# Last head of an encoder's even layer: four output tiles of head 6 go between and behind the levels of head 7's recurrence

## The chip, the cores and the metric

The kernel runs on one core of a Trainium2 chip. The metric is the device time of one execution in microseconds (us); the number that counts is the median of several runs. The five engines of a core run their own instruction streams and meet only at semaphores: TensorE (PE, with its weight loads shown apart as PEld), VectorE (DVE), ScalarE (ACT), GpSimd (POOL, unused here) and SyncE (SP), which issues the DMA transfers.

## The reference

A sequence of 512 positions with 1024 features passes through one even and one odd layer, in float32:

```python
x = x + even_layer(x); x = x + odd_layer(x); return rmsnorm(x)

def even_layer(x):                       # 8 heads in each of two groups
    proj = rmsnorm(x) @ w_in             # 9 sections of 8 heads x 128 columns
    oa = differential_attention(qa, ka, va) * silu(ga)      # dense, two softmaxes
    ob = hgrn2_bidirectional(qh, ff, fb, ih) * silu(gh)     # gated linear recurrence
    return concatenate([oa, ob]) @ w_out
```

The recurrence decays a state by a gate at every position. Both directions are computed here without a state: decayed query-key products for all pairs of positions, times the values.

## The kernel before

Everything is held transposed: features on the 128 partitions, the 512 positions along the free axis. The residual stream is `xT`, eight tiles of 128x512. Each float32 product that must be exact is made of three fast ones (`split_product`, L74 to L76): both operands are split into a high part (rounded to fp32r) and the rest, and high x high, high x low and low x high are summed in a PSUM bank. ACT makes the high part of each weight (`high`, L569, `high_out`, L575), DVE the low part (`low`, L987, `low_out`, L992).

The even layer runs as an iteration for each head h, 0 to 7, with its order written out by hand on each engine; iteration 0 and iteration 7 (`last`) are written out apart, 1 to 6 are a hardware loop. An iteration does, in PE's order: projections 2 to 6 of head h (`proj`), with the attention scores and the transposes of the softmax mix (`turn_mix` 0 to 3) between them; **the eight output tiles of head h-1** (`out_tiles`: each is y of the recurrence and of the attention times one 128-column slice of w_out, so six matmuls of 512 columns in one PSUM bank, which DVE then adds to `xT`, `add_out`, L863); then head h's recurrence: `diagonal` (L443), the attention's `values` (L415, they need all four `keep_mix` of ACT, L629), `far` (L460), and the seven levels `near_level` 0 to 6 (L468). Each level is a chain through three engines: DVE forms differences of decays (L973 to L976), ACT exponentiates them (`near_decays`, L672), DVE multiplies by the query (`near_scale`, L980), PE makes eight matmuls of 128 columns, and ACT (levels 0 and 1, L682) or DVE (levels 2 to 6, `place_level`, L1003) places the result in `attT`. The banks S[0] and S[1] alternate, so level i also waits until level i-2 is placed. In heads 0 to 6, projections 7 to 10 for the next head stand between the levels. In head 7 there is no next head, and nothing stands there.

After iteration 7 comes head 7's end: `recurrence_values` (L415, attT times the values), its square (ACT L595), the sum over partitions (`sum_squares`, L421), a root (ACT L602, L604), `normalize` (DVE L871), `gate_and_split` (DVE L880, L885, L887, which writes the high and low part of y), head 7's eight output tiles, and with them the squares and their sum for the odd layer's norm (L92 to L106).

In iteration 7 before the change, PE runs turn_mix 3, then output tiles 4 to 7 of head 6, then the diagonal. The tiles use two banks in turn, W (`bank_wide`) and O (`bank_out`); `y`, `o_hi` and `o_lo` are one buffer each, so the split weights of head 7's w_out can't be written until tile 7 of head 6 has read the old ones:

```python
def high_out(h, m):                      # ACT
    act.wait_ge(o_in.sem, o_in.at(h, m + 1))
    if O.full.due(h, 5):
        act.wait_ge(O.full.sem, O.full.at(h, 5))
```

Of the kernel before, what the change touches and what calls it, by code (L numbers as in the profile page):

```python
# [153 lines left out]
def even_layer(nc, w_raw, w_hi, w_lo, wn, rstd, xT, eye, ones, rope, eps, x, w_in, w_out, norm, lam, subln, hgw,  # L154
               rope_d, levels_d, eye_d, w_in_next, norm_next):
    with ExitStack() as ctx:
# [113 lines left out]

        block = ctx.enter_context(nc.Block())
# [85 lines left out]
        def _(pe):  # L357
# [52 lines left out]
            def values(h, use, vals, probsT):  # L410

                if O.free.due(h, use - 1):
                    pe.wait_ge(O.free.sem, O.free.at(h, use - 1))
# [9 lines left out]
            def out_tiles(h, js):  # L423
# [3 lines left out]
                for j in js:  # L427
                    bank, use = (W, j // 2 + 1) if j % 2 == 0 else (O, j // 2 + 2)
                    pe.wait_ge(bank.free.sem, bank.free.at(h, use - 1))
                    for m in range(2):  # L430
                        if m == 1:
                            pe.wait_ge(y_hg.sem, y_hg.at(h, 3))
                        mm = split_product(pe, bank[:], o_hi[:, m, j * P:(j + 1) * P], o_lo[:, m, j * P:(j + 1) * P],
                                           y[:, m, 0], y[:, m, 1], m == 0, m == 1)
# [51 lines left out]
            def iteration(h, first, last):  # L486
# [23 lines left out]
                if not first:  # L510
                    out_tiles(h, range(4, 8))
# [12 lines left out]
                if not last:  # L524
                    proj(h, 8)
                near_level(h, 2)
                near_level(h, 3)
# [16 lines left out]
            sum_squares(HEADS, 0, 1)  # L544
            out_tiles(HEADS, range(8))
# [4 lines left out]
        def _(act):  # L550
# [20 lines left out]
            def high_out(h, m):  # L571
                act.wait_ge(o_in.sem, o_in.at(h, m + 1))
                if O.full.due(h, 5):
                    act.wait_ge(O.full.sem, O.full.at(h, 5))
                act.activation(o_hi[:, m], o_raw[:], ACT.Copy).then_inc(o_high.sem, 1)  # L575
# [14 lines left out]
            def square(h, use, n):  # L590
                act.wait_ge(O.full.sem, O.full.at(h, use))
# [115 lines left out]
            def iteration(h, first, last):  # L707
# [25 lines left out]
                keep_mix(h, 2)  # L733
                silu(h, 6, gate_a)
                act.preload_act_table_set(EXP_LOG)
                keep_mix(h, 3)
# [32 lines left out]
            for j in range(KT):  # L769
                act.wait_ge((W, O)[j % 2].free.sem, (W, O)[j % 2].free.at(HEADS, j // 2 + 1 + j % 2))  # L770
# [5 lines left out]
        def _(dve):  # L776
# [81 lines left out]
            def add_out(h, js):  # L858
                for j in js:
                    bank, use = (W, j // 2 + 1) if j % 2 == 0 else (O, j // 2 + 2)  # L860
                    dve.wait_ge(bank.full.sem, bank.full.at(h, use))
                    dve.wait_ge((W if j % 2 == 0 else O).free.sem, (W if j % 2 == 0 else O).free.at(h, use - 1))
                    dve.tensor_tensor(xT[:, j], xT[:, j], bank[:], ALU.add).then_inc(bank.free.sem, 1)  # L863

            def normalize(h, m):

                use, n, w = (1, 1, w_hg) if m else (6, 2, w_sub)
# [6 lines left out]
            def gate_and_split(h, m):  # L874

                use, gate, count, factor = (1, gate_h, y_hg, 1.0) if m else (6, gate_a, y_da, 1.0 - LAM_INIT)
                dve.wait_ge(O.free.sem, O.free.at(h, use))
# [5 lines left out]
                if O.full.due(h, -1 if m else 5):  # L883
                    dve.wait_ge(O.full.sem, O.full.at(h, -1 if m else 5))
                dve.tensor_copy(y[:, m, 0], yn[:]).then_inc(count.sem, 1)  # L885
# [1264 lines left out]
```

## Time and profile before

| | |
|---|---|
| median of 3 runs | 1221.31 us (1219.17 to 1221.83) |
| the profiled execution | 1219.43 us, its span 1217.5 us |
| busy share of the span | PE 95%, PEld 76%, DVE 78%, ACT 55%, POOL 0% |
| granted TensorE clock, mean | 0.982 of full |
| DMA | 103.07 MB, mean 85 GB/s |
| from turn_mix 3 of head 7 to the start of the odd layer | 687.6 to 743.8 us |

The granted clock is given as a share of full speed: 1.00 is 2.4 GHz, 0.50 is 1.2 GHz. A busy PE is not PE at its peak, because matmuls overlap and their ends are modelled. So the pace of PE is read from the starts of its instructions, not from their durations. Stretches of the timeline are what matters here: it lists the instructions of each engine in order of time, merged where one follows the other without a gap, and behind a row the idle time ahead of it and whose event ended it.

### The profile page before, as it was taken

The numbers are of one execution on the slowest core, as the hardware profiler recorded it, in microseconds if no ns is written. First come the engines' busy times: TensorE is split into PE (matmuls) and PEld (weight loads), VectorE is DVE, ScalarE is ACT, GpSimd is POOL, SyncE is SP. The second block draws the span as 40 slices with busy tenths as digits, with TensorE's granted clock in tenths as the row PEclk, the third lists the DMA queues.
The fourth block names the chain that finished last, engine by engine and source line by source line (L and its number), as shares of the span: only waits on it lengthen the run. The fifth ranks groups of instructions, "written<-read, shape, count | busy, mean of one in ns | idle before, by whom it ended". The sixth has DMA issues, their size and how long they took to land. (4 is left out here: it accounts for less than half of the span.)

```text
span 1217.5 us, 18538 instructions
## 1 busy us (share of the span) xinstructions
PE 1155.3 (95%) x5750; PEld 930.0 (76%) x5750; DVE 953.1 (78%) x1882; ACT 666.4 (55%) x1299; POOL 0.2 (0%) x4
## 2 busy tenths in 40 slices
PE   5989999999999999999999967988999999999996
PEld 3867778778778778787887745877888888888876
DVE  5677779778878878877797777577788788888886
ACT  4355455455554554654555544365666665656663
POOL 0000000000000000000000000000000000000000
PEclk9998999999999999999999988998999999999998
DMA  6522521522423225215215003522432223323111
GB/s 194 142 78 56 130 63 53 138 64 65 129 69 91 86 64 138 65 41 136 69 52 139 18 18 92 121 87 65 120 93 52 86 52 103 89 87 86 52 35 70
DMA packets 131672, 103.07 MB, mean 85 GB/s; under 512 B 5424, under 2 KB 116400, under 8 KB 131632
## 3 DMA queue, kind: packets, MB, share of 16 engines
q1 hardware_dynamic: 131632, 102.54, 30.9%
q8 instruction: 24, 0.39, 0.1%
q14 instruction: 16, 0.13, 0.0%
HBM read 77.36 MB, written 2.10 MB: 65 GB/s over the span
## 5 line engine op out<-in xcount | busy, mean ns | idle before, releaser
L74 PE MATMUL bank_proj<-hH,w_hi 128*128 128x512 f32 x576 | 231.0, 401 | 3.8 <-DVE hL L140 3.8
L76 PE MATMUL bank_proj<-hH,w_lo 128*128 128x512 f32 x576 | 226.2, 393 | 0.0
L75 PE MATMUL bank_proj<-hL,w_hi 128*128 128x512 f32 x576 | 225.6, 392 | 0.0
L74 PEld LDWEIGHTS bank_proj<-hH,w_hi 128*128 128x128 f32 x576 | 109.3, 190 | 26.5 <-issue 5.3
L76 PEld LDWEIGHTS bank_proj<-hH,w_lo 128*128 128x128 f32 x576 | 108.9, 189 | 23.8
L75 PEld LDWEIGHTS bank_proj<-hL,w_hi 128*128 128x128 f32 x576 | 109.3, 190 | 21.6
L74 PE MATMUL bank_odd_proj<-hH,w_hi 128*128 128x512 f32 x288 | 117.2, 407 | 5.1 <-DVE hL L140 4.4
L75 PE MATMUL bank_odd_proj<-hL,w_hi 128*128 128x512 f32 x288 | 113.6, 394 | 0.0
L76 PE MATMUL bank_odd_proj<-hH,w_lo 128*128 128x512 f32 x288 | 113.5, 394 | 0.0
L987 DVE TENSOR_TENSOR w_lo<-w_raw,w_hi 128x1024 fp32r<-128x1024 f32 x73 | 88.8, 1218 | 16.9 <-ACT w_hi L569 16.9
L569 ACT ACTIVATE w_hi<-w_raw 128x1024 fp32r<-128x1024 f32 x75 | 78.9, 1054 | 36.8 <-DMA w_raw<-in_w_in_even 33.1
L1591 ACT ACTIVATE probsT<-bank_odd_turn 128x256 fp32r<-128x256 f32 (+1 forms) x128 | 49.3, 435 | 87.1 <-PE bank_odd_turn L1342 86.9
L1584 ACT ACTIVATE probs<-bank_odd_score,small 128x256 f32<-128x256 f32 (+1 forms) x128 | 66.3, 525 | 53.4 <-DVE small L1809 53.4
L616 ACT ACTIVATE probs<-bank_score,small 128x512 f32<-128x512 f32 x64 | 43.4, 684 | 76.3 <-DVE small L836 76.3
L1816 DVE TENSOR_TENSOR probsT<-bank_odd_turn,probsT 128x256 fp32r<-128x256 f32 (+1 forms) x128 | 56.9, 485 | 26.8 <-ACT probsT L1591 26.0
L74 PEld LDWEIGHTS bank_odd_proj<-hH,w_hi 128*128 128x128 f32 x288 | 55.3, 192 | 16.1 <-DVE hL L140 5.2
L468 PE MATMUL bank_score<-scaled 128*128 128x128 f32 x448 | 60.7, 287 | 4.6 <-DVE scaled L980 2.7
L468 PEld LDWEIGHTS bank_score<-scaled 128*128 128x128 f32 x448 | 58.6, 201 | 8.1 <-DVE scaled L980 3.9
L1327 PE MATMUL bank_odd_score<-ks,qs 128*128 128x256 f32 (+1 forms) x256 | 64.2, 355 | 0.0
L76 PEld LDWEIGHTS bank_odd_proj<-hH,w_lo 128*128 128x128 f32 x288 | 54.6, 190 | 12.3
L75 PEld LDWEIGHTS bank_odd_proj<-hL,w_hi 128*128 128x128 f32 x288 | 55.0, 191 | 9.5
L672 ACT ACTIVATE scaled<-decay 128x1024 f32<-128x1024 f32 x32 | 33.9, 1059 | 47.2 <-PE bank_score L468 45.5
(316 smaller groups left out, 2445.4 us busy)
## 6 DMA issues: line engine op xcount, KB each, us to landing
w_raw<-in_w_in_even SPq DMA_DIRECT2D x72, 512.0 KB, 4.7
w_raw<-in_w_in_odd SPq DMA_DIRECT2D x36, 512.0 KB, 4.9
qs<-parts SPq DMA_DIRECT2D x96, 128.0 KB, 2.3
ks<-parts SPq DMA_DIRECT2D x40, 256.0 KB, 4.3
o_raw<-in_w_out_even SPq DMA_DIRECT2D x16, 512.0 KB, 4.8
o_raw<-in_w_out_odd SPq DMA_DIRECT2D x14, 512.0 KB, 6.7
out<-w_raw SPq DMA_DIRECT2D x8, 256.0 KB, 2.1
mixT<-in_x SPq DMA_DIRECT2D x2, 512.0 KB, 5.5
```

Source lines behind the costliest of these rows:

```text
L74: pe.matmul(out, hi, moving_hi, start=start, stop=False)
L75: pe.matmul(out, hi, moving_lo, start=False, stop=False)
L76: return pe.matmul(out, lo, moving_hi, start=False, stop=stop)
L468: mm = pe.matmul(S[i % 2][:, c * P:(c + 1) * P], scaled[:, i % 2, 0, c * P:(c + 1) * P], scaled[:, i % 2, 1, c * P:(c + 1) * P], start=Tru ...
L569: act.activation(w_hi[s][:], w_raw[s][:], ACT.Copy).then_inc(w_high.sem, 1)
L616: act.activation(probs[:, c], S[c][:], ACT.Exp, bias=neg_max[:, i:i + 1], scale=SCALE, accum_out=row_sum[:, i:i + 1]).then_inc(S[c].free.s ...
L672: act.activation(scaled[:, i % 2], buf(i)[:, :, :], ACT.Exp).then_inc(near_exp.sem, 1)
L987: dve.tensor_tensor(w_lo[s][:], w_raw[s][:], w_hi[s][:].bitcast(F32), ALU.subtract).then_inc(w_low.sem, 1)
L1327: mm = pe.matmul(at, query, keys, start=part == 0, stop=False)
L1584: act.activation(probs[:, t % 2, a, 0:n * P], S[a][:, 0:n * P], ACT.Exp, bias=neg_max[:, i:i + 1], scale=SCALE, accum_out=row_sum[:, i:i + ...
L1591: act.activation(probsT[:, 0, 0:n, a], chunked(T[a][:, 0:n * P]), ACT.Copy).then_inc(probs_high[a].sem, 1)
L1816: dve.tensor_tensor(probsT[:, 1, 0:n, a], chunked(T[a][:, 0:n * P]), probsT[:, 0, 0:n, a].bitcast(F32), ALU.subtract).then_inc(T[a].free.s ...
```

## The change

On PE, in iteration 7, head 6's output tiles 4 to 7 no longer stand ahead of the diagonal. Tile 4 comes between levels 1 and 2, tile 5 between levels 2 and 3, and tiles 6 and 7 behind `sum_squares` of head 7's end. DVE adds tiles 4 and 5 to `xT` between placing levels 3 and 4, and tiles 6 and 7 behind head 7's last `gate_and_split`. Banks: tile 5 goes to PB[1], tile 7 to PB[2], 4 and 6 to W; head 7's own even tiles go to O and its odd ones to W. Since head 6's operands are read longer, head 7 gets other homes: its split w_out goes to the memory of `ks`, `qs` and `parts`, the attention half of its y to `hH[:, 0:2]`; the recurrence half of y stays in `y[:, 1]`, and its writing waits for tile 7 (PB[2].full). ACT's `high_out` waits for the last scores (S[1].full) where it waited for tile 7. In iteration 7 ACT also runs `keep_mix(3)` ahead of `silu` of the attention's gate and of the change of activation tables behind it. SP's queue and the DMAs are as they were.

```diff
@@ -268,6 +268,25 @@
         def buf(i):
             return decay if i % 2 == 0 else soft
 
+        def final(h, first=HEADS - 1):
+            return isinstance(h, int) and h >= first
+
+        def o_use(h, n):
+
+            return n - 2 if final(h, HEADS) or final(h) and n > 3 else n
+
+        def out_bank(h, j):
+
+            if final(h, HEADS):
+                return (O, o_use(h, j // 2 + 2)) if j % 2 == 0 else (W, j // 2 + 1)
+            if final(h) and j >= 4:
+                return {4: (W, 3), 5: (PB[1], 3), 6: (W, 4), 7: (PB[2], 3)}[j]
+            return (W, j // 2 + 1) if j % 2 == 0 else (O, j // 2 + 2)
+
+        last_hi = ks[:, :, :, :].rearrange("p c i t -> p (c i t)").rearrange("p (m d) -> p m d", m=2)
+        last_lo = [tile[:, :, :].rearrange("p i t -> p (i t)") for tile in (qs, parts)]
+        last_y = hH[:, 0:2]
+
         block = ctx.enter_context(nc.Block())
 
 
@@ -409,6 +428,7 @@
 
             def values(h, use, vals, probsT):
 
+                use = o_use(h, use)
                 if O.free.due(h, use - 1):
                     pe.wait_ge(O.free.sem, O.free.at(h, use - 1))
                 for c in range(NC):
@@ -425,13 +445,16 @@
                 pe.wait_ge(y_da.sem, y_da.at(h, 0))
                 pe.wait_ge(o_low.sem, o_low.at(h, 0))
                 for j in js:
-                    bank, use = (W, j // 2 + 1) if j % 2 == 0 else (O, j // 2 + 2)
-                    pe.wait_ge(bank.free.sem, bank.free.at(h, use - 1))
+                    bank, use = out_bank(h, j)
+                    pe.wait_ge(bank.free.sem, bank.free.at(HEADS - 1 if bank in PB else h, use - 1))
+                    cols = slice(j * P, (j + 1) * P)
                     for m in range(2):
                         if m == 1:
                             pe.wait_ge(y_hg.sem, y_hg.at(h, 3))
-                        mm = split_product(pe, bank[:], o_hi[:, m, j * P:(j + 1) * P], o_lo[:, m, j * P:(j + 1) * P],
-                                           y[:, m, 0], y[:, m, 1], m == 0, m == 1)
+                        hi, lo = (last_hi[:, m], last_lo[m]) if final(h, HEADS) else (o_hi[:, m], o_lo[:, m])
+                        part = last_y if final(h, HEADS) and m == 0 else y[:, m]
+                        mm = split_product(pe, bank[:], hi[:, cols], lo[:, cols], part[:, 0], part[:, 1],
+                                           m == 0, m == 1)
                     mm.then_inc(bank.full.sem, 1)
 
             def diagonal(h):
@@ -507,7 +530,7 @@
                 turn_mix(h, 2)
                 proj(h, 6)
                 turn_mix(h, 3)
-                if not first:
+                if not first and not last:
                     out_tiles(h, range(4, 8))
 
                 diagonal(h)
@@ -523,7 +546,11 @@
                 near_level(h, 1)
                 if not last:
                     proj(h, 8)
+                else:
+                    out_tiles(h, [4])
                 near_level(h, 2)
+                if last:
+                    out_tiles(h, [5])
                 near_level(h, 3)
                 if not last:
                     proj(h, 9)
@@ -542,6 +569,7 @@
             iteration(HEADS - 1, False, True)
             recurrence_values(HEADS)
             sum_squares(HEADS, 0, 1)
+            out_tiles(HEADS - 1, [6, 7])
             out_tiles(HEADS, range(8))
             rms_next.sum(pe)
 
@@ -570,9 +598,11 @@
 
             def high_out(h, m):
                 act.wait_ge(o_in.sem, o_in.at(h, m + 1))
-                if O.full.due(h, 5):
+                if final(h):
+                    act.wait_ge(S[1].full.sem, S[1].full.at(h, 4))
+                elif O.full.due(h, 5):
                     act.wait_ge(O.full.sem, O.full.at(h, 5))
-                act.activation(o_hi[:, m], o_raw[:], ACT.Copy).then_inc(o_high.sem, 1)
+                act.activation((last_hi if final(h) else o_hi)[:, m], o_raw[:], ACT.Copy).then_inc(o_high.sem, 1)
 
             def soften(h, d):
 
@@ -588,7 +618,7 @@
                 act.activation(at, at, ACT.Ln, bias=1.0).then_inc(softplus.sem, 1)
 
             def square(h, use, n):
-                act.wait_ge(O.full.sem, O.full.at(h, use))
+                act.wait_ge(O.full.sem, O.full.at(h, o_use(h, use)))
                 act.wait_ge(T.full.sem, T.full.at(h, 7 - 8 if n == 1 else 1))
                 if squared.due(h, n - 1):
                     act.wait_ge(squared.sem, squared.at(h, n - 1))
@@ -731,9 +761,12 @@
                 silu(h, 4, query)
                 silu(h, 5, gate_h)
                 keep_mix(h, 2)
+                if last:
+                    keep_mix(h, 3)
                 silu(h, 6, gate_a)
                 act.preload_act_table_set(EXP_LOG)
-                keep_mix(h, 3)
+                if not last:
+                    keep_mix(h, 3)
                 high_out(h, 0)
                 high(h, 9)
                 square(h, 6, 2)
@@ -767,7 +800,8 @@
             square(HEADS, 1, 1)
             root(HEADS, 0, 1)
             for j in range(KT):
-                act.wait_ge((W, O)[j % 2].free.sem, (W, O)[j % 2].free.at(HEADS, j // 2 + 1 + j % 2))
+                bank, use = out_bank(HEADS, j)
+                act.wait_ge(bank.free.sem, bank.free.at(HEADS, use))
                 rms_next.square(act, j)
             rms_next.root(act)
 
@@ -857,14 +891,15 @@
 
             def add_out(h, js):
                 for j in js:
-                    bank, use = (W, j // 2 + 1) if j % 2 == 0 else (O, j // 2 + 2)
-                    dve.wait_ge(bank.full.sem, bank.full.at(h, use))
-                    dve.wait_ge((W if j % 2 == 0 else O).free.sem, (W if j % 2 == 0 else O).free.at(h, use - 1))
+                    bank, use = out_bank(h, j)
+                    at = HEADS - 1 if bank in PB else h
+                    dve.wait_ge(bank.full.sem, bank.full.at(at, use))
+                    dve.wait_ge(bank.free.sem, bank.free.at(at, use - 1))
                     dve.tensor_tensor(xT[:, j], xT[:, j], bank[:], ALU.add).then_inc(bank.free.sem, 1)
 
             def normalize(h, m):
 
-                use, n, w = (1, 1, w_hg) if m else (6, 2, w_sub)
+                n, w = (1, w_hg) if m else (2, w_sub)
                 dve.wait_ge(rooted.sem, rooted.at(h, n))
                 if (y_da if m else y_hg).due(h, 0 if m else 3):
                     dve.wait_ge((y_da if m else y_hg).sem, (y_da if m else y_hg).at(h, 0 if m else 3))
@@ -874,17 +909,22 @@
             def gate_and_split(h, m):
 
                 use, gate, count, factor = (1, gate_h, y_hg, 1.0) if m else (6, gate_a, y_da, 1.0 - LAM_INIT)
-                dve.wait_ge(O.free.sem, O.free.at(h, use))
+                to = last_y if final(h) and m == 0 else y[:, m]
+                dve.wait_ge(O.free.sem, O.free.at(h, o_use(h, use)))
                 bank, gate_use = bank_of(5 if m else 6)
                 dve.wait_ge(bank.free.sem, bank.free.at(h, gate_use - (3 if m else 0)))
                 dve.scalar_tensor_tensor(out=yn[:], in0=yn[:], scalar=factor, in1=gate[:], op0=ALU.mult,
                                          op1=ALU.mult).then_inc(count.sem, 1)
                 dve.wait_ge(count.sem, count.at(h, 1))
-                if O.full.due(h, -1 if m else 5):
+                if final(h, HEADS):
+                    dve.wait_ge(PB[2].full.sem, PB[2].full.at(HEADS - 1, 3))
+                elif final(h) and m == 0:
+                    dve.wait_ge(PB[2].full.sem, PB[2].full.at(h, 2))
+                elif O.full.due(h, -1 if m else 5):
                     dve.wait_ge(O.full.sem, O.full.at(h, -1 if m else 5))
-                dve.tensor_copy(y[:, m, 0], yn[:]).then_inc(count.sem, 1)
+                dve.tensor_copy(to[:, 0], yn[:]).then_inc(count.sem, 1)
                 dve.wait_ge(count.sem, count.at(h, 2))
-                dve.tensor_tensor(y[:, m, 1], yn[:], y[:, m, 0].bitcast(F32), ALU.subtract).then_inc(count.sem, 1)
+                dve.tensor_tensor(to[:, 1], yn[:], to[:, 0].bitcast(F32), ALU.subtract).then_inc(count.sem, 1)
 
             def rotate(h, n):
 
@@ -989,8 +1029,8 @@
 
             def low_out(h, m):
                 dve.wait_ge(o_high.sem, o_high.at(h, m + 1))
-                dve.tensor_tensor(o_lo[:, m], o_raw[:], o_hi[:, m].bitcast(F32),
-                                  ALU.subtract).then_inc(o_low.sem, 1)
+                hi, lo = (last_hi[:, m], last_lo[m]) if final(h) else (o_hi[:, m], o_lo[:, m])
+                dve.tensor_tensor(lo, o_raw[:], hi.bitcast(F32), ALU.subtract).then_inc(o_low.sem, 1)
 
             def place_level(h, i):
 
@@ -1037,7 +1077,7 @@
                 mixes(h, 3)
                 low(h, 8)
                 far_scale(h)
-                if not first:
+                if not first and not last:
                     add_out(h, range(4, 8))
                 place_diagonal(h)
                 near_differences(h, 0)
@@ -1066,6 +1106,8 @@
                 if not last:
                     low(h, 11)
                     rotate(h, 8)
+                else:
+                    add_out(h, [4, 5])
                 place_level(h, 4)
                 near_scale(h, 6)
                 place_level(h, 5)
@@ -1080,6 +1122,7 @@
             iteration(HEADS - 1, False, True)
             normalize(HEADS, 1)
             gate_and_split(HEADS, 1)
+            add_out(HEADS - 1, [6, 7])
             for j in range(KT):
                 add_out(HEADS, [j])
                 if j >= 2:
```

## Rows read from the trace of the kernel before

**Rows 1.** Windows: length, busy PE, PEld, DVE, ACT, POOL; granted clock; DMA share

```profile
700.00:743.80 43.80, 30.17 (x124) 21.91 (x122) 30.73 (x57) 20.55 (x34) 0.00 (x0) 0.88 0.04 12
...
706.00:708.00 2.00, 1.55 (x7) 1.56 (x8) 2.00 (x6) 1.93 (x5) 0.00 (x0) 0.54 0.00 0
...
716.00:718.00 2.00, 1.43 (x10) 0.97 (x8) 1.35 (x3) 0.67 (x1) 0.00 (x0) 0.90 0.00 0
...
726.00:728.00 2.00, 0.00 (x0) 0.00 (x0) 1.90 (x4) 0.00 (x0) 0.00 (x0) 1.00 0.00 0
```

**Rows 2.** Timeline, PE: turn_mix 3, first matmul of tile 4, diagonal, values

```profile
687.60 0.60 PE L392 MATMUL bank_turn<-eye,mix 128*128 128x128 f32 x4
687.95 0.48 PE L74 MATMUL bank_wide<-y,o_hi 128*128 128x512 f32 x1
...
693.52 1.05 PE L443 MATMUL bank_score<-query,attT 128*128 128x128 f32 x8
...
694.55 3.67 PE L415 MATMUL bank_out<-mixT,v 128*128 128x512 f32 x8
```

**Rows 3.** Timeline, ACT, over the same stretch

```profile
687.79 0.60 ACT L634 ACTIVATE gate_a<-bank_proj 128x512 f32<-128x512 f32 x1 [2.48 <-PE bank_proj L76]
688.41 1.28 ACT L735 ACT_TABLE_LOAD   x1
689.70 0.60 ACT L629 ACTIVATE mixT<-bank_turn 128x512 f32<-128x512 f32 x1
693.77 1.06 ACT L575 ACTIVATE o_hi<-o_raw 128x1024 fp32r<-128x1024 f32 x1 [3.47 <-PE bank_out L76]
...
694.74 1.04 ACT L569 ACTIVATE w_hi<-w_raw 128x1024 fp32r<-128x1024 f32 x1
...
698.26 0.60 ACT L595 ACTIVATE sq<-bank_out 128x512 f32<-128x512 f32 x1 [2.48 <-PE bank_out L415]
```

**Rows 4.** Timeline, DVE: last part of far_scale, placing the diagonal

```profile
686.26 0.87 DVE L950 TENSOR_SCALAR scaled<-scaled,small 128x128 f32<-128x128 f32 x4
...
694.61 0.69 DVE L941 TENSOR_TENSOR attT<-bank_score,eye 128x512 f32<-128x512 f32 x1 [0.20 <-PE bank_score L443]
```

**Rows 5.** Timeline, PE: level 1; levels 2 and 3; levels 4 and 5

```profile
703.84 1.16 PE L468 MATMUL bank_score<-scaled 128*128 128x128 f32 x8 [0.79 <-DVE scaled L980]
...
706.45 4.20 PE L468 MATMUL bank_score<-scaled 128*128 128x128 f32 x16 [1.44 <-DVE scaled L980]
...
712.52 3.76 PE L468 MATMUL bank_score<-scaled 128*128 128x128 f32 x16 [1.88 <-DVE attT L1003]
```

**Rows 6.** Timeline, ACT and DVE between the levels

```profile
705.71 0.68 DVE L980 TENSOR_TENSOR scaled<-query,scaled 128x512 f32<-128x512 f32 x1
...
707.35 1.11 ACT L682 ACTIVATE attT<-bank_score 32x128 f32<-32x128 f32 x4
...
710.74 1.06 ACT L672 ACTIVATE scaled<-soft 128x1024 f32<-128x1024 f32 x1 [1.06 <-DVE decay L973]
...
712.27 0.68 DVE L980 TENSOR_TENSOR scaled<-query,scaled 128x512 f32<-128x512 f32 x1
...
714.67 1.06 ACT L672 ACTIVATE scaled<-decay 128x1024 f32<-128x1024 f32 x1 [2.87 <-PE bank_score L468]
714.75 0.73 DVE L1003 COPY_PREDICATED attT<-level_mask,bank_score 128x512 f32<-128x512 uint8 x1 [1.17 <-PE bank_score L468]
```

**Rows 7.** Timeline: head 7's values, sum of squares, split of y, first adds

```profile
718.62 3.70 PE L415 MATMUL bank_out<-attT,vh 128*128 128x512 f32 x8 [0.96 <-DVE attT L1003]
...
723.10 1.10 PE L421 MATMUL bank_turn<-sq,ones 128*128 128x512 f32 x2 [0.78 <-ACT sq L595]
...
727.13 0.43 DVE L885 CAST y<-yn 128x512 fp32r<-128x512 f32 x1
...
729.34 0.69 DVE L863 TENSOR_TENSOR xT<-xT,bank_wide 128x512 f32<-128x512 f32 x1 [1.05 <-PE bank_wide L76]
...
730.71 0.69 DVE L863 TENSOR_TENSOR xT<-xT,bank_out 128x512 f32<-128x512 f32 x1 [0.69 <-PE bank_out L76]
```

## The prediction

> **What bounds the kernel now.** I looked at the page first: PE is busy 95% of the span, so most of it is a queue of matmuls in which reordering gains nothing. The slices show one hole before the odd layer, and the windows give it an edge: from 700.0 to 743.8 us PE is busy 30.17 of 43.80 us, and DVE and ACT aren't full either [rows 1]. So there the time is set by a chain through the engines, and 13.6 us of PE are free. Just ahead of the hole, PE is full. The timeline of that stretch shows what it is full of: turn_mix 3 from 687.60, head 6's tiles 4 to 7 from 687.95, and only at 693.52 the diagonal with which head 7's recurrence begins on PE [rows 2]. DVE has had its scaled operands ready since 686.26 + 0.87 = 687.13 and waits for the diagonal, which it places at 694.61 [rows 4]. ACT waits 3.47 us for tile 7 [rows 3]. The chain of this stretch is therefore: four tiles on PE, diagonal, values, square, far products, seven levels, head 7's values, square, sum, root, y, eight tiles, norm. Whatever can leave the front of it and fit into its holes is gained whole.
>
> **The front: tiles 4 to 7 leave.** They are 24 matmuls, and their price is the distance of the starts: 693.52 − 687.95 = 5.57 us, 0.232 each, 1.39 a tile [rows 2]. The diagonal moves to 687.95. What could be late there instead:
>
> - DVE has nothing pending after 687.13, so placing the diagonal moves from 694.61 to 689.04 [rows 4]. The adds of tiles 4 to 7 are gone from there too.
> - PE's `values` moves from 694.55 to 688.98 [rows 2] and needs `keep_mix(3)`. In the old ACT order it would wait: the silu, the table change, and then the copy, which ends at 689.70 + 0.60 = 690.30 [rows 3], 1.3 us late. In the new order the copy comes first. The transposes end at 687.60 + 0.60 = 688.20 [rows 2], so it runs from about 688.24 to 688.84: 0.1 us ahead of need.
> - Behind it ACT runs the silu (0.60), the table change (1.28), the split of head 7's w_out (its successor starts 694.74 − 693.77 = 0.97 later) and the split of a weight of the odd layer (1.04), and then the square, which PE's values now want at 698.26 − 5.57 = 692.69 [rows 3]. From 688.73 that is: silu to 689.35, change to 690.63, split to 691.61, split to 692.65. It just fits, with nothing to spare: 0 us, and each 0.1 us more in this row of five is 0.1 us on the path.
>
> ACT's old wait for tile 7 is replaced by one for the last scores, long past; the homes in `ks`, `qs`, `parts` and `hH` are free then, since head 7 has no next head to rotate and its last projection is done before turn_mix 3. No instruction is added for them. SP issues what it did, with head 7's second w_out load 5.6 us sooner on idle DMAs. The front gives −5.57 us.
>
> **The activation tables, weighed.** The row shows a table change of 1.28 us with the next ACT instruction 0.01 us behind it (688.41 + 1.28 = 689.69, then 689.70) and none but the usual gap ahead of it [rows 3]. The Trainium skill, "ScalarE: Activation LUTs", section "What ACT_TABLE_LOAD costs", gives about 1283 ns for the load and a drain of about 1380 ns beside it, some 2.66 us for each switch. The load agrees with the trace, the drain does not appear in it. By the page the ACT row above would be 1.38 us longer and the gain only about 4.2 us; by the row it costs nothing more.
>
> **Tile 4, between levels 1 and 2.** Level 1's eight matmuls start at 703.84 and PE then sits idle 1.44 us until level 2 at 706.45, which waits for DVE's multiply (705.71 + 0.68 = 706.39) [rows 5, 6]. I put these in the old times, all of which move by −5.57. PE can issue the tile at about 703.84 + 1.0 = 704.84 and is through with its issue at 706.23: inside the hole, 0 us.
>
> **Tile 5, between levels 2 and 3.** Level 3 waits for ACT to place level 1 (707.35 + 1.11 = 708.46) [rows 6]. At full clock level 2 is issued by 707.45 and the tile by 708.84, so level 3 is 0.3 us late. Who waits for it: ACT's exponentials of level 5, at 710.74 [rows 6]. Their reader on DVE comes at 712.27 whatever they do, because DVE's differences and a placement stand ahead of it, and they last 1.06: ready at 711.80, 0.47 us of cover. So 0 us. In the old trace levels 2 and 3 took 4.20 us for 16 matmuls at a clock of 0.54 to 0.50 in place of some 2.2 [rows 1, 5]; see the rivals.
>
> **Adds of tiles 4 and 5** are two DVE instructions of 0.69 [rows 7], some 1.3 us issued back to back, ahead of placing level 4. DVE is idle 1.17 us there before [rows 6]; so that placement is 0.1 us late. The next in line, level 6's multiply, waits for ACT's exponentials until 714.67 + 1.06 = 715.73, and the placement ends before it: 0 us.
>
> **Tiles 6 and 7, behind the sum of squares.** Sum_squares ends on PE at 723.10 + 1.10 = 724.20 with its issue done a little sooner [rows 7]. Twelve matmuls at 0.232 take 2.8 us: the last ends at about 727.0. DVE writes the high part of y at 727.13 [rows 7], and it now waits for tile 7: 0.1 us of cover. PE then makes the attention half of head 7's tile 0 (three matmuls, 0.7 us, on bank O, which the normalize has left before the multiply that ends ahead of 727.13) by 727.7, before y is complete at 729.34 − 1.05 = 728.29. Two more adds of 0.69 on DVE start at 728.29, and the first add of head 7's tiles comes at about 729.5 in place of 729.34. The next has 0.69 us of idle time ahead of it [rows 7], which takes this in: 0 to 0.2 us, I take 0.1. Bank W is freed for tile 1 by 728.29 + 0.69 = 728.98, and PE wants it behind the second half of tile 0, at 728.3 + 0.7 = 729.0: just in time.
>
> **Sum.** −5.57 + 0 + 0 + 0 + 0.1 = −5.5 us (rounded) on the profiled execution: 1219.43 − 5.5 = 1213.9. That execution was 1.9 us below the median of the runs, which I take as chance; against the median, **1221.31 − 5.5 = 1215.8 us**.
>
> **Unknowns and their bounds.** What the trace of before doesn't show is how these tiles go with the clock. Before, the clock fell to half in 706 to 708, after PE's thin stretch, and rose in 716 to 718; through 726 to 728, with PE wholly idle, it stayed at 1.00 [rows 1]. With tiles 4 and 5 PE is nearly unbroken from 703.8 to 710, and the first fall should be gone; between level 3's end and level 4's start at 712.52 is a hole of about 2.5 us that stays [rows 5]. The lower bound of cost is full clock throughout: levels 4 and 5 then take 2.3 us (twice 1.16) in place of 3.76 [rows 5]. Level 4 ends 0.7 earlier, but DVE is now the limit, since the adds come first, from 714.75 − 1.17 = 713.58 to about 714.8 [rows 6], and the placement ends at 715.4, 0.35 us ahead of where the multiply began before: about −0.4 us. The upper bound is half clock from level 2 on: level 2 in 1.9, tile 5 in 2.8, level 3 in 1.9, so level 3 ends at 713.0 in place of 710.65, the exponentials of level 5 end 2.3 us late where 0.47 was covered, and what follows catches up in part with DVE's idle 1.17: +1.1 us. Both ends are kept; I take 0, by the row nearest: levels 4 and 5 as slow as before, 2 and 3 faster.
>
> **Rivals.**
>
> 1. *As summed*, −5.0 to −6.1 us, about 1215.8: 0.62.
> 2. *Full clock to the end*: −5.5 − 0.4 and a little from a luckier clock elsewhere, −6.3, 1215.0. For it: no fall in 726 to 728 without any matmul. Against: the fall near 706 with PE still over half busy. 0.12.
> 3. *Half clock in levels 2 to 5 or late into level 6*: −5.5 + 1.1 to + 2.5, so −3 to −4.4, 1217.6. For it: rows 5. 0.13.
> 4. *ACT becomes the front's bound*: the row of five has no slack; if the change of tables costs a drain in its new place, +1.3, so −4.2, 1217.1. Against: the row shows none. 0.05.
> 5. *The tiles don't fit, and the change gives back what it takes*: if PE can't issue tiles 6 and 7 before `normalize` or the sum's bank, they stand on the path with 2.8 us, and tile 5 with 1.4: −1.3, 1220.0, no difference that can be told. Against: the holes were read at 1.44 and, with rows 7, nearly 3 us. 0.05.
> 6. *Slower*: the clock falls in the hole before level 4 and isn't given back until after tiles 6 and 7. Level 6 costs +0.7, the values' 3.70 us double, +3.7, sum_squares +0.9, and the two tiles 5.6 us in place of 2.8, which pushes the high part of y by 2.6: +7.9, so +2.4, and head 7's first tiles more: 1224. It decides from a cost of 5.5, that is from a half clock that lasts until tile 7. Against: the rise at 716 to 718 before the values [rows 1]. 0.03.
>
> **How the numbers follow.** 1215.8 is case 1. Runs of this kernel lie 1.4 us either side of their middle, so 0.2% (2.4 us) is about what can be told from no change. The range runs from full clock with a good draw, 1213.4, to case 3's dear end, 1218.5, and leaves out cases 5 and 6 and a tail at both sides, in all under 0.2. Faster by over 0.2%: cases 1 to 4 whole, 0.92; the same: case 5, 0.05; slower: case 6, 0.03.
>
> **What would show it.** In the changed profile: the diagonal right behind turn_mix 3, and values 1.0 us behind it with no wait for ACT; the square of the attention right at the end of values; level 2 still released by DVE, not by tile 4; DVE's idle time before level 4's placement gone; the high part of y released by ACT's root, not by tile 7; the start of the odd layer near 738.3 in place of 743.8. From turn_mix 3 to there the distance shrinks by 5.5 us and nothing else moves. Wrong it would be by a wait on ACT's copy or square, by level 3 behind tile 5 at half clock, or by the high part of y waiting for PE.

## The result, and the profile after

The changed kernel takes 1212.64 us at the median of six runs (1211.01 to 1215.56), the kernel before 1219.49 us (1219.11 to 1221.83): 6.9 us less, ratio 0.994 with a 95% interval of 0.9925 to 0.9956, so 5.4 to 9.2 us. The forecast was faster, which held, at 1215.8 us with a range from 1213.4, which did not: the measured time lies 0.8 us below its low end. The profiled execution took 1211.01 us with a span of 1209.1, and 8.4 us of span is more than the medians differ by. So the first question to the profile is where the 8.4 us lie. The timeline of PE after, in the rows that answer to [rows 2], [rows 5] and [rows 7]:

```profile
682.83 0.60 PE L411 MATMUL bank_turn<-eye,mix 128*128 128x128 f32 x4
683.26 1.06 PE L466 MATMUL bank_score<-query,attT 128*128 128x128 f32 x8
684.15 3.66 PE L435 MATMUL bank_out<-mixT,v 128*128 128x512 f32 x8
...
696.04 1.16 PE L491 MATMUL bank_score<-scaled 128*128 128x128 f32 x8
...
698.42 1.05 PE L491 MATMUL bank_score<-scaled 128*128 128x128 f32 x8
...
702.00 2.34 PE L491 MATMUL bank_score<-scaled 128*128 128x128 f32 x16 [2.52 <-DVE attT L1043]
...
707.62 5.40 PE L435 MATMUL bank_out<-attT,vh 128*128 128x512 f32 x8 [0.96 <-DVE attT L1043]
713.79 1.10 PE L441 MATMUL bank_turn<-sq,ones 128*128 128x512 f32 x2 [0.78 <-ACT sq L625]
```

The sum of the next norm on PE, and the odd layer's first multiply on DVE, which is the start of the odd layer in the prediction; first the kernel before, then after:

```profile
741.01 1.12 PE L106 MATMUL bank_turn<-rstd,ones 128*128 128x512 f32 x2 [2.18 <-DVE rstd L101]
743.84 1.42 DVE L136 SCALAR_TENSOR_TENSOR soft<-xT,wn,rstd 128x512 f32<-128x512 f32 x2 [2.88 <-PEq L156]
```

```profile
731.72 1.97 PE L106 MATMUL bank_turn<-rstd,ones 128*128 128x512 f32 x2 [2.18 <-DVE rstd L101]
735.40 1.41 DVE L136 SCALAR_TENSOR_TENSOR soft<-xT,wn,rstd 128x512 f32<-128x512 f32 x2 [3.74 <-PEq L156]
```

Read as distances from turn_mix 3 of head 7 (687.60 before, 682.83 after):

| from turn_mix 3 to | before | after |
|---|---|---|
| diagonal | 5.92 | 0.43 |
| attention's values | 6.95 | 1.32 |
| head 7's values | 31.02 | 24.79 |
| its sum of squares | 35.50 | 30.96 |
| the sum of the next norm | 53.41 | 48.89 |
| the odd layer's first multiply (DVE) | 56.24 | 52.57 |

Turn_mix 3 itself comes 4.77 us earlier, in code that the change doesn't touch. From there to the odd layer the stretch is 3.67 us shorter, where the forecast wanted 5.5, and the two make up the 8.4. The front gives 5.63 us by the values, where 5.57 were forecast. By head 7's values it is 6.23 us. Behind them 1.7 is lost again, because those eight matmuls take 5.40 us in place of 3.70, and another 0.85 at the norm's sum, which takes 1.97 us in place of 1.12. The windows say why. From 60 to 105 us (head 0), from turn_mix 3 to head 7's values, and from there to the next norm's sum, first the kernel before, then after; the number ahead of the two of the DMA is the granted clock:

```profile
60.00:105.00 45.00, 39.23 (x159) 28.77 (x158) 31.64 (x69) 26.04 (x51) 0.00 (x0) 0.89 0.28 84
687.60:718.62 31.02, 25.45 (x120) 20.15 (x118) 23.73 (x49) 17.99 (x28) 0.00 (x0) 0.83 0.05 17
718.62:741.01 22.39, 15.99 (x59) 10.67 (x59) 15.14 (x23) 6.97 (x11) 0.00 (x0) 1.00 0.00 1
```

```profile
60.00:105.00 45.00, 38.75 (x184) 29.91 (x183) 34.77 (x75) 27.14 (x52) 0.00 (x0) 1.00 0.28 82
682.83:707.62 24.79, 19.02 (x108) 14.47 (x106) 21.76 (x47) 17.87 (x28) 0.00 (x0) 1.00 0.06 21
707.62:731.72 24.10, 20.45 (x71) 13.51 (x71) 16.23 (x25) 6.98 (x11) 0.00 (x0) 0.93 0.00 1
```

At 0.83 of full over 31.02 us, the clock before was at its lower level, 1.2 GHz, for about 10 us; after, it isn't at all in the levels, and it is for some 3.4 us in head 7's values. Ahead of that fall PE was busy 3.42 us of the 7.5 from 700.0 to 707.5, all at full clock. Some of the rows at half a us, with the fall and the rise, after:

```profile
707.00:707.50 0.50, 0.00 (x0) 0.00 (x0) 0.50 (x2) 0.00 (x0) 0.00 (x0) 1.00 0.00 0
707.50:708.00 0.50, 0.39 (x1) 0.30 (x2) 0.50 (x2) 0.00 (x0) 0.00 (x0) 0.97 0.00 0
708.00:708.50 0.50, 0.50 (x2) 0.18 (x1) 0.50 (x1) 0.00 (x0) 0.00 (x0) 0.50 0.00 0
...
711.00:711.50 0.50, 0.50 (x2) 0.21 (x1) 0.00 (x0) 0.00 (x0) 0.00 (x0) 0.61 0.00 0
```

Head 0, which both kernels run alike, had in 60 to 105 us about 10 us of the lower clock before and none after. Its turn_mix 3, the attention's values and the far products, first before, then after:

```profile
90.57 0.63 PE L392 MATMUL bank_turn<-eye,mix 128*128 128x128 f32 x4 [2.49 <-ACT mixT L629]
...
92.88 6.51 PE L415 MATMUL bank_out<-mixT,v 128*128 128x512 f32 x8 [0.58 <-ACT mixT L629]
99.23 1.91 PE L460 MATMUL bank_score<-scaled 128*128 128x128 f32 x10
```

```profile
88.59 0.63 PE L411 MATMUL bank_turn<-eye,mix 128*128 128x128 f32 x4 [2.54 <-ACT mixT L659]
...
90.90 3.70 PE L435 MATMUL bank_out<-mixT,v 128*128 128x512 f32 x8 [0.79 <-ACT mixT L659]
94.43 1.91 PE L483 MATMUL bank_score<-scaled 128*128 128x128 f32 x10
```

After is 1.98 us ahead at this turn_mix 3 and 4.80 us ahead behind the values. That is a draw, since other runs of the same code show either value (6.50 us in "two between", 3.70 in "homes only"), and it is the whole of the early 4.77 us. The two front steps that had no slack went as forecast; the rows of ACT that answer to [rows 3]:

```profile
683.46 0.60 ACT L659 ACTIVATE mixT<-bank_turn 128x512 f32<-128x512 f32 x1 [2.89 <-PE bank_turn L411]
683.96 0.59 ACT L664 ACTIVATE gate_a<-bank_proj 128x512 f32<-128x512 f32 x1
684.57 1.28 ACT L767 ACT_TABLE_LOAD   x1
685.86 1.06 ACT L605 ACTIVATE ks<-o_raw 128x1024 fp32r<-128x1024 f32 x1
686.82 1.04 ACT L597 ACTIVATE w_hi<-w_raw 128x1024 fp32r<-128x1024 f32 x1
...
687.85 0.60 ACT L625 ACTIVATE sq<-bank_out 128x512 f32<-128x512 f32 x1
```

The copy comes first, the table change is 1.28 us with no drain behind it, and the square starts without a wait. By the Trainium skill's "ScalarE: Activation LUTs", section "What ACT_TABLE_LOAD costs", a drain of about 1.38 us would have delayed it; again no row shows one.

### The profile page after: what moved, and what is told of

Same layout as the page of the kernel before. It is cut to its first block and busy times, and to the rows that moved or that the text cites. A ratio compares the mean times of both kernels' runs of the same rounds, so it can differ in the third digit from the quotient of the medians.

```text
span 1209.1 us, 18540 instructions
## 1 busy us (share of the span) xinstructions
PE 1148.0 (95%) x5750; PEld 923.7 (76%) x5750; DVE 952.1 (79%) x1882; ACT 666.5 (55%) x1299; POOL 0.2 (0%) x4
## 5 line engine op out<-in xcount | busy, mean ns | idle before, releaser
L491 PE MATMUL bank_score<-scaled 128*128 128x128 f32 x448 | 57.3, 276 | 4.8 <-DVE attT L1043 2.5
L491 PEld LDWEIGHTS bank_score<-scaled 128*128 128x128 f32 x448 | 55.5, 191 | 8.3 <-DVE scaled L1020 3.2
```

Of the source, the lines that this page charges most:

```text
L491: mm = pe.matmul(S[i % 2][:, c * P:(c + 1) * P], scaled[:, i % 2, 0, c * P:(c + 1) * P], scaled[:, i % 2, 1, c * P:(c + 1) * P], start=Tru ...
```

## The experiments

The question: is the gain beyond 5.5 us structure that the sum missed, clock, or a draw? One run of "6, 7 behind" took 4030 us, with no known cause; it is in no median and no ratio here. Medians, all against the kernel before on the same chip. Distances are from turn_mix 3 of head 7 in each profile, and each row of the table has one profile.

| kernel | median us (runs) | before us | ratio, 95% interval |
|---|---|---|---|
| homes only | 1217.89 (12) | 1218.14 | 0.9997, 0.9978 to 1.0016 |
| 6, 7 behind | 1213.78 (11) | 1218.14 | 0.9960, 0.9941 to 0.9980 |
| two between | 1215.38 (12) | 1218.14 | 0.9978, 0.9959 to 0.9997 |
| old copy order | 1212.71 (12) | 1218.14 | 0.9951, 0.9931 to 0.9971 |
| before, filled | 1215.54 (11) | 1219.73 | 0.9962, 0.9951 to 0.9973 |
| after, filled | 1209.21 (6) | 1219.73 | 0.9913, 0.9896 to 0.9930 |
| after, filled in head 7 | 1210.29 (6) | 1219.73 | 0.9934, 0.9909 to 0.9958 |
| after, head 0's copies | 1209.38 (6) | 1219.73 | 0.9912, 0.9894 to 0.9929 |
| after again | 1210.01 (6) | 1218.48 | 0.9938, 0.9917 to 0.9959 |
| before, short fillers | 1212.57 (8) | 1218.48 | 0.9953, 0.9937 to 0.9970 |
| after, short fillers | 1207.09 (5) | 1218.48 | 0.9907, 0.9888 to 0.9927 |
| combined | 1205.43 (5) | 1218.48 | 0.9892, 0.9871 to 0.9912 |
| after, short, adds later | 1207.20 (4) | 1218.36 | 0.9910, 0.9883 to 0.9936 |
| combined, adds later | 1206.47 (4) | 1218.36 | 0.9905, 0.9880 to 0.9929 |

**Homes only.** PE and DVE order as before, all else as changed; one of several places:

```diff
-                if not first and not last:
+                if not first:
                     out_tiles(h, range(4, 8))
```

> The changed kernel with tiles 4 to 7 of head 6 back ahead of the diagonal (adds too); new homes, banks, waits and the earlier keep_mix(3) stay. Theory (the gain is the four tiles leaving the front, 5.57 us, plus clock): the same as before, within 0.5 us, apart from the draw of the clock. Rival (the homes themselves or the earlier wait of ACT give a part of the 6.9 us): 1 to 1.4 us faster than before.

No difference in the time that can be told: the interval runs from 2.7 us faster to 1.9 slower, so it does not by itself exclude the rival's 1 to 1.4 us. The profile speaks against the rival: head 7's values are 0.22 us earlier than before (30.80 and 31.02), the next norm's sum 0.61 later (54.02 and 53.41). It shows a price that I had not seen: head 7's tile 0 is on bank O now and waits for the normalize, which leaves PE idle, and here the clock was at its lower level behind that hole (0.53 in 721 to 723 us):

```profile
720.00 0.75 DVE L901 SCALAR_TENSOR_TENSOR yn<-bank_out,w_hg,rstd 128x512 f32<-128x512 f32 x1 [4.15 <-ACT rstd L629]
...
720.90 0.56 PE L74 MATMUL bank_out<-hH,ks 128*128 128x512 f32 x1 [2.32 <-DVE yn L901]
721.26 0.63 PE L75 MATMUL bank_out<-hH,ks 128*128 128x512 f32 x1
```

In the full change tiles 6 and 7 stand there, and 0.69 us of the hole is left.

**Only tiles 6 and 7 behind; only two tiles between.** Tiles 4 and 5 stay ahead of the diagonal; the other two go behind the sum of squares, or between the levels:

```diff
-                if not first and not last:
-                    out_tiles(h, range(4, 8))
+                if not first:
+                    out_tiles(h, range(4, 6) if last else range(4, 8))
```

> Tiles 6 and 7 behind the sum of squares as in the change, tiles 4 and 5 back ahead of the diagonal. Theory: half of 5.57, so 2.8 us faster than before, with levels 2 to 5 at half clock as before. Rival (filling the levels is worth more than the tiles' own time, by the clock): this one gains less than half of what the whole change gains, about 2.5 us.

> Tiles 6 and 7 between the levels, where the change has 4 and 5; tiles 4 and 5 ahead of the diagonal; nothing behind the sum of squares. Theory by issue time alone: 2.8 us faster than before. Rival (clock): 2.8 plus 0.6 to 1 us, since levels 2 to 5 run at full clock; the profile then shows the clock at 1.00 from level 2 to level 3.

The profiles give 2.86 us each at the attention's values (4.09 in place of 6.95), half the front. The times give 4.4 and 2.8 by the medians, 4.9 and 2.7 by the ratios, and add up to the whole. Neither rival is told apart by them; the intervals are 2 us wide each way. The profiles do say something of the second. With two tiles between, levels 2 and 3 ran at full clock (1.16 and 1.05 us), levels 4 and 5 did not (3.46 us for 16 matmuls), and head 7's values are 3.34 us earlier than before, 0.5 more than the half front. By the next norm's sum it is 2.48, since tile 0 waits there as in "homes only"; with 6 and 7 behind it is 3.01. The two add up to 5.49 us.

**The old copy order.**

```diff
-                if last:
-                    keep_mix(h, 3)
                 silu(h, 6, gate_a)
                 act.preload_act_table_set(EXP_LOG)
-                if not last:
-                    keep_mix(h, 3)
+                keep_mix(h, 3)
```

> The changed kernel with keep_mix(3) behind the silu and the table change again. Theory: values wait for the copy, 1.3 to 1.4 us later than in the changed kernel, so a gain over before of 5.5 in place of 6.9 us. Rival (ACT has cover there): the same as the changed kernel.

```profile
684.13 1.06 PE L466 MATMUL bank_score<-query,attT 128*128 128x128 f32 x8
...
686.45 3.70 PE L435 MATMUL bank_out<-mixT,v 128*128 128x512 f32 x8 [1.27 <-ACT mixT L659]
```

The wait of 1.27 us for ACT's copy is there, and values start at 2.76 in place of 1.32: 1.44 us. The time alone (6.0 us faster by the ratio) could not have shown it.

**Fillers.** To take the clock out of the comparison, PE gets idle matmuls in its holes, on constants and into banks that nobody reads. They stand in head 0, between head 7's levels, in its end and at the odd layer's start; this is one of the places:

```diff
+            def fill(bank, n):
+                for _ in range(n):
+                    pe.matmul(bank[:, 0:P], ones, eye[:], start=True, stop=True)
...
                 if not last:
                     proj(h, 9)
+                else:
+                    fill(PB[0], 14)
                 near_level(h, 4)
```

> The kernel before, with idle matmuls of 128 columns on constants, into banks nobody reads, in PE's holes of head 0, head 7's levels, its end and the start of the odd layer; the output is unchanged. They are sized to end inside the holes. Theory (the clock is worth some us in this kernel, drawn anew in each run): faster than before by 3 to 6 us and with less spread, because 2.8 us at head 0's values and about 2 us at the odd layer's start, both seen at half clock, go. Rival (the holes are short enough, the clock doesn't matter): the same or slower by the fillers that don't fit.

> The changed kernel with the same fillers, less those whose holes the tiles fill. Theory (structure 5.57 us, the rest is clock): 5.5 us faster than the filled kernel before, since both are at full clock, and 4 us faster than the changed kernel. Rival (the surplus of 1.3 us is structure that I missed): 6.9 us faster than the filled kernel before.

> The changed kernel with fillers in head 7 and at the odd layer's start alone, none in head 0. Theory: most of the filled kernel's gain, 2 to 3 us over the changed kernel, with the spread that head 0's draw gives (up to 4.7 us between runs) left. Rival: all of it is head 0's, no difference to the changed kernel.

Filled, the kernel before gains 4.2 us, and the two filled kernels are 6.3 us apart. But my fillers were twice as long as meant. In the filled changed kernel the 14 ahead of level 4 are 28 records, two passes each, and level 4 starts behind them, not behind DVE:

```profile
699.87 3.29 PE L427 MATMUL bank_proj<-eye,ones 128*128 128x128 f32 x28
...
703.00 1.95 PE L495 MATMUL bank_score<-scaled 128*128 128x128 f32 x16
```

So the 6.3 hold overruns of either kernel. From turn_mix 3 to the odd layer's first projection the two profiles are 6.31 us apart (61.30 and 54.99). Fillers in head 7 alone left the spread of the runs at 1207.2 to 1216.1 us, those in head 0 as well 1207.0 to 1211.0, which points to head 0 for the spread, by six runs of each. The changed kernel without fillers did not run on that chip, so what these two gain over it is not told. With about half of them:

> The kernel before with fillers of half the number: each of them turned out to be two passes of 0.12 us, so the first set ran over its holes by about 0.8 us in head 7 alone. Theory: full clock throughout, the overrun gone, so about 1 to 2 us faster than the first filled kernel before, some 5 to 6 us faster than before. Rival: shorter fillers no longer hold the clock, and the gain shrinks.

> The changed kernel with the shorter fillers. Theory (structure): 5.6 us faster than the kernel before with the shorter fillers, in the time and in the distance from turn_mix 3 to the norm's sum in the profiles. Rival (structure I missed): 6.5 us or more.

The windows of the two from turn_mix 3 to head 7's values, before and after:

```profile
683.36:713.34 29.98, 26.36 (x157) 21.21 (x156) 23.56 (x49) 18.01 (x28) 0.00 (x0) 1.00 0.05 18
```

```profile
681.72:706.51 24.79, 22.15 (x135) 17.60 (x134) 21.76 (x47) 17.89 (x28) 0.00 (x0) 1.00 0.07 22
```

The times are 1212.57 and 1207.09: 5.5 us, as the sum had it, with about 1.2 us either way by the spread of the runs. The profiles give 5.14 by the odd layer's first multiply (55.19 and 50.05). Full clock alone takes 1.04 us from the kernel before in this stretch (31.02 to 29.98) and nothing from the changed one, which had it. At the attention's values the filled kernels are 5.62 us apart (6.95 and 1.33), at head 7's values 5.19.

**The change again, and its adds later.** The change once more beside the kernel before:

> The changed kernel itself, once more, beside the same runs of the kernel before. The kernel before has spread over 1213.6 to 1223.2 us in 35 runs, so a median of six runs of each is uncertain by a us or more. Theory (structure 5.6 us, and about 1 us of clock that the filled levels save): 6 to 7 us faster than before, median near 1212 to 1213. Rival (the 6.9 us of the first comparison were a draw): 5.0 to 5.5 us.

Between the two: 8.5 us by these medians, 7.6 by the ratio, with an interval of 5.0 to 10.1 us. Both lie beyond the 6 to 7 us of the theory, and the interval takes in the rival's 5.0 to 5.5 too. Of the kernel before there are 77 runs in all, 1213.6 to 1223.2 us with a mean of 1218.6; twelve of the change have a mean of 1211.3. That is 7.3 us, with about 1.7 either way, and it mixes chips, on which the means of the kernel before run from 1217.9 to 1220.1. In the profile of this second set the stretch to the odd layer's first multiply is 5.74 us shorter than before (50.50 and 56.24). The 0.43 us given back between 5.62 and 5.19 is looked for on DVE:

```diff
-                else:
-                    add_out(h, [4, 5])
                 place_level(h, 4)
...
                 if last:
                     gate_and_split(h, 0)
+                    add_out(h, [4, 5])
```

> The changed kernel with the shorter fillers, and DVE's adds of tiles 4 and 5 moved from ahead of level 4's placement to behind head 7's attention gate. At full clock the two filled kernels are 5.62 us apart at the attention's values, but only 5.19 at head 7's values. Theory (the two adds stand on DVE's path at full clock): head 7's values start at turn_mix 3 + 24.35 in place of 24.79, the norm's sum 0.4 earlier as well. Rival (the 0.43 is lost elsewhere, on PE behind tile 5): 24.79 stays.

The kernel before with short fillers, then the changed one with the adds in place, then with them moved (both with short fillers):

```profile
709.48 0.75 DVE L1022 COPY_PREDICATED attT<-level_mask,bank_score 128x512 f32<-128x512 uint8 x1 [0.25 <-PE bank_score L472]
```

```profile
701.84 0.67 DVE L914 TENSOR_TENSOR xT<-xT,bank_wide 128x512 f32<-128x512 f32 x1
...
702.43 0.68 DVE L914 TENSOR_TENSOR xT<-xT,bank_proj 128x512 f32<-128x512 f32 x1
703.03 0.73 DVE L1059 COPY_PREDICATED attT<-level_mask,bank_score 128x512 f32<-128x512 uint8 x1
703.65 0.68 DVE L1036 TENSOR_TENSOR scaled<-query,scaled 128x512 f32<-128x512 f32 x1
```

```profile
704.50 0.74 DVE L1059 COPY_PREDICATED attT<-level_mask,bank_score 128x512 f32<-128x512 uint8 x1 [0.24 <-PE bank_score L495]
705.50 0.69 DVE L1036 TENSOR_TENSOR scaled<-query,scaled 128x512 f32<-128x512 f32 x1 [0.27 <-ACT scaled L718]
```

With the adds in place DVE has no idle time and level 6's multiply queues behind the placement; with them moved it waits for ACT, as before the change. Head 7's values start at 24.35 in place of 24.79, 0.44 us. The idle time on which the forecast laid the adds (1.17 us, [rows 6]) was made for the most part by PE's half clock; at full clock it is 0.25.

**Head 0's copies, and the versions put together.** Where PE waits for ACT in head 0, the copies of the mix go ahead:

```diff
+                if first:
+                    keep_mix(h, 2)
                 silu(h, 4, query)
                 silu(h, 5, gate_h)
-                keep_mix(h, 2)
-                if last:
+                if not first:
+                    keep_mix(h, 2)
+                if first or last:
                     keep_mix(h, 3)
...
-                if not last:
+                if not first and not last:
                     keep_mix(h, 3)
```

> The changed kernel with ACT's copies of the mix in head 0 ahead of what they stood behind: keep_mix(2) ahead of the two silus and keep_mix(3) ahead of the third silu and the table change. In head 0 PE waits 2.5 us for the one and 0.6 to 0.8 us for the other. Theory: 2 to 3 us faster than the changed kernel, and less clock lost at head 0's values. Rival (silu of the query, now 0.5 us later, becomes what diagonal and far products wait for): under 1 us.

> The changed kernel, head 0's copies of the mix in their new order, and the shorter fillers: the version that the runs so far point to. Theory: head 0's order gives 2 to 3 us whatever the clock, the fillers 3 to 4 us; together 12 to 14 us faster than before, near 1206. Rival (both cure the same loss, the half clock at head 0's values): about 10.5 us, no better than either alone.

> The combined version with the adds of tiles 4 and 5 later too. Theory: 0.4 us faster than the combined version, near 1205.0; below what the times alone can tell, but the profile's distances can. Rival: no difference.

Head 0's order is 10.3 us faster than before at the median. In its profile PE's wait ahead of the diagonal is 1.24 us in place of the 2.5 us ahead of turn_mix 3:

```profile
89.47 1.13 PE L466 MATMUL bank_score<-query,attT 128*128 128x128 f32 x8 [1.24 <-issue]
```

It was not run with the changed kernel on the same chip, but its profile gives its own share: from head 0's turn_mix 2 to its far products 12.58 us (81.36 to 93.94) in place of 14.50 (79.93 to 94.43 in the changed kernel, both with the values at full clock), 1.9 us. The combined version has the lowest median, 1205.4, 13 us under before and 1.7 under the filled changed kernel beside it. Its fillers differ in one place: four behind head 0's turn_mix 3 in place of nine ahead of it. The 12 to 14 us of the theory held; the order's share is 1.7 to 1.9 us, a little under the 2 to 3 of the theory. Later adds show in its profile (values at 24.34) and not in its time.

## Why the prediction was right and where it failed

- *The front, −5.57.* Right: 5.63 us at the attention's values in the profile, 5.62 at full clock. DVE, `keep_mix(3)` and ACT's row of five behaved as summed; a copy left behind costs 1.44 us where 1.3 was said.
- *Tiles 4 and 5 at nothing.* Right by the profile: head 7's values are not later than the front's gain allows, and with the adds out of the way the full-clock distances (29.98 and 24.35) differ by 5.63, all of the front.
- *The adds of 4 and 5 at nothing.* Wrong at full clock, 0.44 us: this term was mis-sized. I named this limit in the bounds and then took the half-clock case.
- *Tiles 6 and 7, +0.1.* Right in kind: at full clock the distance from head 7's values to the next norm's sum is 22.38 before and 22.44 after. The high part of y starts in the profile after at 717.82, and the last matmul of tile 7 ended at 717.66 (717.27 + 0.39).
- *The clock at 0.* Mis-sized too, at the step "0, by the row nearest: levels 4 and 5 as slow as before". In the profile after, levels 2 to 5 all ran at full clock, and by head 7's values the stretch gave 6.23 us in place of 5.5; in the changed kernel's second profile it gave 5.74, with levels 4 and 5 slow (3.44 us) and the clock at 0.93. The first is rival 2, which had 0.12, but only as far as the levels: in head 7's values the lower clock came, +1.7 us, and again at the norm's sum, +0.85. In the second profile both ran at full clock. Slow values of head 7 stand in two more profiles without fillers (5.26 us with the old copy order, 5.99 with head 0's copies). Over the whole stretch to the odd layer the two profiles give 3.67 and 5.74 us, so the clock there did not give the surplus: it cost 1.8 us in the one and gave 0.2 in the other.
- *The level and the range.* This is the step that put the time outside. The sum was taken from 1221.31, the median of three runs, and the low end, 1213.4, stood on "1.4 us either side of their middle". The 77 runs of the kernel before spread over 9.7 us with a mean of 1218.6. The median that the time was measured against moved from 1221.31 to 1219.49 by itself, 1.8 us, and the surplus over the sum is 1.4: together the 3.2 us by which the forecast missed. From 1219.49 the same sum gives 1214.0, and the same range 1211.6 to 1216.7, which holds the measured 1212.64. The profiled execution before, 1219.43, whose lower time I put down to chance, was the better guide to the level: from there I had 1213.9.
- *"Nothing else moves."* The sign that I named, turn_mix 3 to the odd layer shorter by 5.5 us and nothing else, failed in the profile after: 3.67 there and 4.77 ahead of it, in head 0. More than half of the 8.4 us between the two profiled executions is thus that draw, and luck.

With the clock at full in both kernels the gain is 5.5 us by the medians and 5.14 by the profiles, which is 5.63 less 0.44 for the adds and 0.06 behind head 7's values. The gain measured without fillers, 6.9 and 7.6 us by the first medians and the second ratio, is larger by 1 to 2 us, but both intervals (5.4 to 9.2, 5.0 to 10.1) reach down to 5.5. By head 7's values the profiles show 1.04 − 0.44 = 0.6 us of saving, one profile of each kernel, and the first loses it again behind them. Whether there is a surplus, and where, stays open.

## What to carry to other kernels

Work that stood ahead of a latency chain and needed nothing from it was worth its full issue time here, 5.63 us, when it was put into the chain's holes, on two conditions: its operands got homes of their own, and the evictions must not take the idle time of the next engine, which cost 0.44 us. Ask of each idle time what made it: one that a slow PE made is gone when PE is faster. A kernel whose runs spread by 10 us should not be judged by three of them; distances between two instructions of one profile settle in hundredths of a us what medians can't, as long as the clock in that stretch is looked at too. And a forecast of a time needs a level as good as its sum: three runs were 1.8 us off.

## What the runs showed of the hardware

- In this kernel the draw of the clock in head 0's attention's values, 2.8 us, is worth half of the change: they took 6.51 us at the lower level and 3.70 at the full one, behind a hole of 2.5 us in both profiles.
- A float32 matmul of 128 columns on constants is two records of 0.12 us, 3.29 us for 14. As fillers they held the granted clock at 1.00 through every hole from turn_mix 3 to the odd layer's first projections, in the profiles of both filled pairs, and with half their number they made both kernels faster, by 5.9 us at the median for the kernel before and 2.9 for the changed one.
